# Feed-forward hand-over split early, low parts of the activation rows moved to VectorE, silu spread over three units, in a two-block transformer kernel

## The reference, cut to what matters

```
# peer, per token: chosen experts of 128*128, g their softmax weights
u = take(expert_down, idx); act = gelu(xi . u)
out = sum_k (g * act)_k * take(expert_up, idx)_k
# modulation of the second block, from the condition rows c and c_ctx
m = silu(c) @ w_mod[l] + b_mod[l]
# feed-forward of the second block, width 2816
swiglu(x) = (silu(x @ wi_a) * (x @ wi_b)) @ wo
```

## Time and profile before

| | us |
|---|---|
| runs of the kernel before | 3290.89, 3312.47, 3317.73 (median 3312.47) |
| the profiled execution | 3297.96, of which its span 3296.3 |

### The profile page before, as it was taken

The page is one execution under the profiler, slowest core; times in us unless marked ns, Lnnn a source line. Parts: engine busy times, 40 slices in busy tenths (PEclk is TensorE's granted clock), DMA queues, the critical chain, the costliest instruction groups (busy, mean ns, idle before and its releaser), DMA issues. The chain is left out here.

```text
span 3296.3 us, 68177 instructions
## 1 busy us (share of the span) xinstructions
PE 3187.2 (97%) x26292; PEld 3114.6 (94%) x26292; DVE 2081.7 (63%) x3335; ACT 1544.6 (47%) x2596; POOL 584.8 (18%) x451
## 2 busy tenths in 40 slices
PE   9899999999999899999999999999998899999998
PEld 9699999999999799999999999999986799999998
DVE  4649698868885649788867775332255455554654
ACT  5244576654444644566655454222144344443343
POOL 0117700033331107700033331000010000000000
PEclk9899999999998999999999998999998799999999
DMA  5145644478896245544489993222250145454453
GB/s 177 55 147 182 186 149 142 157 250 279 276 348 210 68 141 175 187 151 145 146 269 316 314 315 132 96 95 96 70 154 26 52 153 187 158 185 159 135 191 128
DMA packets 178908, 560.42 MB, mean 170 GB/s; under 512 B 22480, under 2 KB 31440, under 8 KB 178144
## 3 DMA queue, kind: packets, MB, share of 16 engines
q1 hardware_dynamic: 178784, 558.82, 51.7%
HBM read 557.71 MB, written 1.05 MB: 170 GB/s over the span
## 5 line engine op out<-in xcount | busy, mean ns | idle before, releaser
L238 DVE TENSOR_TENSOR peer_e_lo<-peer_raw,peer_e_hi 128x1024 fp32r<-128x1024 f32 x430 | 537.7, 1250 | 275.8 <-ACT peer_e_hi L234 275.2
L234 ACT ACTIVATE peer_e_hi<-peer_raw 128x1024 fp32r<-128x1024 f32 x512 | 539.3, 1054 | 333.1 <-PE peer_e_out L1269 330.8
L238 DVE TENSOR_TENSOR ffn_lo<-ffn_raw,ffn_hi 128x1024 fp32r<-128x1024 f32 x256 | 313.0, 1225 | 478.9 <-ACT ffn_hi L234 478.9
L234 ACT ACTIVATE ffn_hi<-ffn_raw 128x1024 fp32r<-128x1024 f32 x264 | 278.7, 1060 | 529.7 <-PE ffn_acc L2484 321.5
L1265 PE MATMUL peer_e_out<-x_normed,peer_e_hi 128*128 128x256 f32 x2048 | 494.8, 283 | 7.0 <-ACT peer_e_hi L234 7.0
L1322 PE MATMUL peer_e_out<-peer_h_pair,peer_e_hi 128*128 128x256 f32 x2048 | 485.6, 278 | 0.9 <-ACT peer_e_hi L234 0.6
L1323 PE MATMUL peer_e_out<-peer_h_pair,peer_e_hi 128*128 128x256 f32 x2048 | 485.6, 278 | 0.0
L1266 PE MATMUL peer_e_out<-x_normed,peer_e_hi 128*128 128x256 f32 x2048 | 483.5, 278 | 0.0
L238 POOL TENSOR_TENSOR peer_h_pair<-peer_e_h,peer_h_pair 128x256 fp32r<-128x256 f32 x256 | 240.2, 939 | 974.2 <-ACT peer_h_pair L234 974.2
L1265 PEld LDWEIGHTS peer_e_out<-x_normed,peer_e_hi 128*128 128x128 f32 x2048 | 386.4, 189 | 7.3 <-ACT peer_e_hi L234 7.3
L1322 PEld LDWEIGHTS peer_e_out<-peer_h_pair,peer_e_hi 128*128 128x128 f32 x2048 | 386.0, 188 | 1.4 <-ACT peer_e_hi L234 0.8
(11 more groups left out here) (638 smaller groups left out, 6647.7 us busy)
## 6 DMA issues: line engine op xcount, KB each, us to landing
peer_raw<-in_l_down SPq DMA_DIRECT2D x256, 512.0 KB, 3.5
peer_raw<-in_l_up SPq DMA_DIRECT2D x256, 512.0 KB, 4.7
ffn_raw<-in_ffn_wi SPq DMA_DIRECT2D x176, 512.0 KB, 3.7
peer_ring<-in_w_mod SPq DMA_DIRECT2D x144, 512.0 KB, 5.2
ffn_raw<-in_ffn_wo SPq DMA_DIRECT2D x88, 512.0 KB, 3.5
l_in_raw<-in_l_w_in SPq DMA_DIRECT2D x39, 512.0 KB, 4.2
peer_q_raw<-in_l_peer_w_query SPq DMA_DIRECT2D x32, 512.0 KB, 4.9
wg_in_raw<-in_w_in SPq DMA_DIRECT2D x26, 512.0 KB, 3.8
```

The source lines that it names most:

```text
L234: return act.activation(hi, v, ACT.Copy)
L238: return eng.tensor_tensor(lo, v, hi.bitcast(F32), ALU.subtract)
```

## The change

1. swiglu: `cut_second` and `low_second` of unit 0 move ahead of the last silu and the last `gate`, those of unit 1 ahead of the last `cut_g` and `low_g`. TensorE's `keep_awake` goes. With two streams, its wait for all gates becomes two waits inside unit 0.
2. up stage of peer_experts: `h_lo` is computed by VectorE (`low_h`), directly ahead of `low_up`, and for unit 0 after the last `use`. GpSimd's loop goes.
3. The silus: unit 7 (`SILU_AT`) gets a silu of one element, unit 8 the first condition row, unit 9 the second (layer 0 alone has it).

```diff
@@ peer_experts, ScalarE
-                if n == 2 * RAWS:
+                if n == SILU_AT:
                     act.wait_ge(cond_in, 16)
-                    act.wait_ge(lo_h, 2 * RAWS)
-                    for c in range(NC):
-                        act.activation(conds[c], ring[:, 2 + c], ACT.Silu).then_inc(silued, 1)
+                    act.activation(dens[:, 0, 0:1], K.eps[:], ACT.Silu)
+                elif SILU_AT < n <= SILU_AT + NC:
+                    c = n - SILU_AT - 1
+                    act.wait_ge(lo_h, 4 * c + 4)
+                    act.activation(conds[c], ring[:, 2 + c], ACT.Silu).then_inc(silued, 1)
@@ peer_experts, GpSimd
-            with pool.Fori(0, BODIES) as i:
-                for k in range(RAWS):
-                    n = i * RAWS + k
-                    pool.wait_ge(hi_h, n + 1)
-                    cut_lo(pool, h_lo[:, k % 2:k % 2 + 1], h[:, bass.ds(n, 1), :], h_hi[:, k % 2:k % 2 + 1])\
-                        .then_inc(lo_h, 1)
@@ peer_experts, VectorE
+            def low_h(n):
+                dve.wait_ge(hi_h, n + 1)
+                cut_lo(dve, h_lo[:, n % 2], h[:, n], h_hi[:, n % 2]).then_inc(lo_h, 1)
...
             low_up(0)
             use(NK - 2)
             use(NK - 1)
+            low_h(0)
             for n in range(1, NK):
+                low_h(n)
                 low_up(n)
@@ swiglu, TensorE
                 for c in range(DC):
+                    if start and n_s == 2 and c in (0, DC // 2):
+                        pe.wait_ge(gated, FT - 1 if c == 0 else FT)
...
-            keep_awake(pe, K, acc[:, 7, 0:P], 6)
-            if n_s == 2:
-                pe.wait_ge(gated, FT)
@@ swiglu, ScalarE
-            silu(FT - 1, 1)
-            for f in (FT - 2, FT - 1):
-                cut_g(f, f % 2)
...
-            for f in range(2):
-                act.wait_ge(product, 2 * FT - 1 + f)
-                cut_second(f, f, 16)
+            act.wait_ge(product, 2 * FT - 1)
+            cut_second(0, 0, 16)
+            silu(FT - 1, 1)
+            cut_g(FT - 2, 0)
+            act.wait_ge(product, 2 * FT)
+            cut_second(1, 1, 16)
+            cut_g(FT - 1, 1)
@@ swiglu, VectorE
-            gate(FT - 1, 1)
-            for f in (FT - 2, FT - 1):
-                low_g(f, f % 2)
...
-            for f in range(2):
-                low_second(f, f)
+            low_second(0, 0)
+            low_g(FT - 2, 0)
+            gate(FT - 1, 1)
+            low_second(1, 1)
+            low_g(FT - 1, 1)
```

More of the change, by code:

```diff
@@ L1132, in peer_experts @@
     MOD_FROM = 3 * RAWS
+    SILU_AT = 2 * RAWS - 1
     with stage(nc, f"{name}_e") as st:
```

## The result

The changed kernel takes 3292.58 us (median of 7 runs, 3286.64 to 3299.21), the kernel before 3312.47 us in the same session (7 runs, 3290.89 to 3331.19). The ratio is 0.9931 with a 95% interval of 0.9907 to 0.9954. A second measurement of both on another chip gave 0.9966 (0.9939 to 0.9994). The profiled execution took 3292.58 us, its span 3290.8.

What follows compares the result with a forecast made beforehand. TensorE, busy 97% of the span, was taken as the bound. Waits of -9.5 - 0.8 + 0 + 2.8 = -7.5 us, then paces of -2.3 and +13.5, took 3297.96 to 3301.7 us, given as 3302; range 3284 to 3320.

Steps and rivals of the forecast that it cites:

- layer 1 falling into the slow pace: Forecast case: the waits go, but layer 1's up stage turns slow at its new entry restart, +13.5 us; chance 0.47.
- Part 1: Feed-forward hand-overs: TensorE's four waits go, 9.5 us together, and nothing else comes late.
- a second phase inherits the pace of the first: Feed-forward ffn2_1: without the hand-over gap its second phase keeps the first's fast pace, -2.3 us.
- Part 2: Silus spread over units 7 to 9: layer 0's up-stage gap of 0.8 us goes, and a restart with it.
- Part 3: Low part of h on VectorE, steady state: 2.72 us a unit, even with TensorE's fast unit; cost taken as 0.
- x: VectorE's time from accumulator read to next start in an up-stage unit, between 0.08 and 0.53 us, taken as 0.08.
- Part 4: Low part of h for unit 0: TensorE waits 1.4 us at each up-stage entry, together 2.8 us.
- The rival that VectorE becomes the bound: Layer 0's up stage: at x of 0.53 us a unit takes 3.17 us, +38 us, 3328 us; chance 0.06.
- Nothing in the change sets the pace; what it changes is where the restarts are: All matmul streams: pace, about 4.4 ns a matmul apart, can change only at TensorE restarts, which the change moves.
- the sum stays: Layer 1's up stage: VectorE regains some 0.09 us a unit from less contention, hidden by TensorE's bound, no gain.
- a restart can settle in either pace: All matmul streams: each TensorE restart may leave either pace, about 4.4 ns apart; a gapless stream keeps its own.
- slow again: Layer 0's up stage: restarting at unit 0 instead of unit 9, if slow again, costs 1 us more.

Runs made afterwards that it cites:

- e2: Kernel before with only the silus spread over units 7 to 9; 3317.8 us, ratio 1.001 to the kernel before.
- e3: Kernel before with only the low part of h moved from GpSimd to VectorE; 3309.45 us, ratio 0.9987.
- e11: The kernel before, unchanged, timed against itself; 3300.12 us, ratio 0.9991.
- e5: Changed kernel plus a useless GpSimd subtraction per row reading two SBUF operands; 3323.07 us, ratio 1.0063 to the kernel before.
- e6: Changed kernel plus a useless GpSimd memset per row, which only writes; 3297.26 us, ratio 0.9963 to the kernel before.
- e8: Changed kernel plus two short idle matmuls at two places of each feed-forward; 3307.33 us, ratio 1.0013 to the kernel before.
- e9: The changed kernel measured once more, in a later session; 3297.54 us, ratio 0.9966 to the kernel before.
- e12: Changed kernel with the silus together at unit 8 again; 3278.05 us, ratio 0.9925 to the kernel before.
- e1: Kernel before with only the feed-forward hand-overs changed; 3310.82 us, ratio 0.9997.
- e4: Changed kernel with the low part of h back on GpSimd, keeping new hand-overs and spread silus; 3306.75 us, ratio 0.9974 to the kernel before.
- e7: e4 plus a useless VectorE product in each layer 1 unit that had none; 3302.19 us, ratio 0.9994 to the kernel before.
- e10: Changed kernel with row 0's low part of h done by GpSimd ahead of time; 3276.19 us, ratio 0.9921 to the kernel before.

## Why the prediction was right, and where it was wrong

The time came out in the range, and faster than before as said, but the sign was luck. The forecast's own terms are -7.5 - 2.3 + 13.5 = +3.7 us, a kernel slightly slower than before. It lies below the median of 3312.47 only because it was added to the profiled execution of 3297.96, which was 14.5 us below that median. The range of 36 us, about 1%, holds nearly every outcome that was weighed. The time of 3302 us was 9.4 us above the measured median; its likeliest case, layer 1 falling into the slow pace, did not occur in any profile of the changed kernel.

- **Part 1** did what was worked out: the four waits are gone, nothing is late next. That a second phase inherits the pace of the first also held, in 40 of 40 phases of the ten profiles with the new hand-over. With the old one, in four profiles (before, e2, e3, e11), 13 first phases were fast and 6 of them were followed by a slow second phase; none of the 3 slow ones recovered. That is about 1.5 phases an execution, some 4 us, where 2.3 were counted.
- **Part 2**: the gap of 0.8 us went. In time nothing of it can be seen.
- **Part 3**: x is about 0 where 0.08 was taken. VectorE's unit is thus 2.64 us by the prediction's own terms, not even with TensorE's 2.72 but 0.08 below it, and the only gap of TensorE behind the entry is 0.35 us ahead of the last unit, where before had 0.25.
- **Part 4**: 1.62 us for each entry, not 1.4. The step from `low_h`'s end to TensorE was taken as 0.05 us, which no row showed, and is 0.25.
- **The rival that VectorE becomes the bound** did not come, and e5 shows how near it is.

**The step that failed** is "Nothing in the change sets the pace; what it changes is where the restarts are", with its companion on the shared port, that the bound of TensorE hides it: "the sum stays". From it came the forecast that layer 1's up stage turns slow at its new entry wait, +13.5 us. It did not: in the seven profiles with that wait (after, e3, e5, e6, e8, e9, e12) all 7 entries of layer 1 were left at the fast pace, and 6 of the 7 of layer 0. The one that was not is e3's, slow for its first nine units. So that a restart can settle in either pace, the other half of the prediction's picture, holds: of the restarts at unit 9, those of before and e1 were left slow and those of e3, e11 and e12 fast. And layer 0's up stage, left at "slow again" by the forecast, became fast, -12.6 us.

What the runs put in its place: the change does set the pace in layer 0, by taking GpSimd's reads of SBUF away. With GpSimd's subtraction in the loop the stage was slow in 6 of 6 profiles (before, e1, e2, e4, e7, e11), by two ways. In before and e1 it was slow from the restart at unit 9, as the prediction read it. In e2, e4, e7 and e11 it was fast at first and lost the pace to contention, each time at unit 19, seven units after the first product. Without that subtraction, and with no other reads by GpSimd, it was fast in 7 of 7 (after, e3, e6, e8, e9, e10, e12) from unit 9 on, in e3 and e12 behind the restart there. So the restart alone, which part 2 removes, was not what had to go: with it gone and GpSimd's reads left (e2, e4), the stage is slow all the same. The earlier trace rows held the sign of it, 1226 ns against 1317 for one instruction. I read it as the gain that layer 1 would get; it says that at the fast pace GpSimd's turn reaches into `low_up`, and at the slow pace hardly. Layer 1 can pay the difference out of VectorE's idle time, layer 0, with a product in nearly each unit, can't.

The sum corrected: -9.5 - 0.8 + 3.2 - 12.6 - 4 = -23.7 us, a ratio of 0.9928. It is made from the profiles, after the fact. The first measurement, 0.9931, agrees; the second, 0.9966 (0.9939 to 0.9994), is less. Which stretch takes part of the gain back isn't known.

What stays open is what decides the pace of a stream at its start. In the 14 profiles ffn1_0's first phase was slow 7 times, ffn2_0's 2, ffn1_1's 5 and ffn2_1's 4, with the same code there but for the two matmuls of e8. That alone moves the total by up to 13.5 us for ffn1_0 and 6.8 us for each of the others. Together with the 16 us by which the stretches outside the up stages and feed-forwards vary, it makes parts worth 10 us hard to see.

## What to carry to other kernels

Divide the length of a gapless window by its matmuls before asking which engine is busy: two stages with TensorE at 100% and the granted clock at 1.00 can differ by 4%. Where VectorE is nearly full, look at whether GpSimd reads SBUF beside it; a VectorE instruction that varies in duration with GpSimd's position is the sign. Compare the ends of the rows, as the start of one that waits for its turn says nothing. An overrun of 0.1 us a unit can cost more than itself, as TensorE leaves its fast pace for the rest of the stream. A move of work from an idle engine to a nearly full one can be a gain for that reason alone, but then its time must be counted to the hundredth: 2.64 us in a unit of 2.72 held here, 3.03 did not. And add a forecast to the same base with which the result will be compared.

## What the runs showed of the hardware

- **Two paces of matmuls of 256 columns with a weight load each**, 113.3 and 117.8 ns, both with a granted clock of 1.00 (the 2.4 GHz level). Streams of up to 3072 matmuls kept their pace to the end where nothing disturbed them. In the up stages a single stall of 0.05 us turned fast into slow for the more than 100 units that followed (e2 from 716.22, layer 1 of e7 from 1708.34). From slow to fast the up stages and feed-forwards changed for good only across restarts (e3 at unit 9). In the second half of the down stages, where eight matmuls of another kind (line 1307) stand between two units, the units are slow and fast in turn (after, 612.8 to 649.6). What decides the pace is open.
- **VectorE and GpSimd take turns when both read SBUF, and the wait is inside their recorded durations.** In e4 `low_up` goes from 1.22 us (696.54) to 1.75 and GpSimd's subtraction from 0.74 to 1.78 (723.12), while their ends keep a fixed distance: GpSimd's end 0.60 us behind that of the product, `low_up`'s 1.09 behind GpSimd's. The Trainium skill (SBUF — State Buffer, "Who interferes with whom") names the condition, a VectorE instruction with two SBUF inputs and a GpSimd one that reads SBUF, and e5 against e6 agrees: the product takes 1614 ns beside reads and 1218 beside a memset. The Trainium skill also says there that the shared port is an exclusive lock, which fits these ends: the rows overlap in the trace, the work doesn't.
- **An accumulator read of VectorE doesn't hold up the next instruction**: in after both carry the time stamp 784.25, and from the product to `low_h` it is 1.15 us, as from `low_up` to the product (784.68 to 785.82, 1.14).
